# First layer's attention: VectorE scales a head's weights before the next head's mask and maximum, from the third step on; one pair's end moves a step

## The reference

```
qf = q * scale
s_own = where(causal, einsum(qf, k_own), NEG_INF)      # 8 heads, 256 x 256
p = softmax(s_own)
out = einsum(p, v_own)
attn = head_rms_norm(merge_heads(out), attn_out_g, 8)
```

## Time and profile before

| | us |
|---|---|
| three runs | 1297.15, 1297.38, 1300.36 |
| median | 1297.38 |
| the profiled execution, whole | 1299.01 |
| its span, first to last instruction | 1297.1 |
| TensorE busy | 1121.5 (86%) |
| VectorE busy | 670.1 (52%) |
| ScalarE busy | 550.3 (42%) |
| mean granted TensorE clock | 0.95 |

### The profile page before, as it was taken

How to read it: one execution, slowest core, us unless ns; L and a number is a source line. 1 busy time by engine, 2 the same in 40 slices (tenths; PEclk the granted TensorE clock), 3 DMA queues, 4 the chain that set the end, 5 groups by cost and what they waited for, 6 DMA issues and landing times.

```text
span 1297.1 us, 20055 instructions
## 1 busy us (share of the span) xinstructions
PE 1121.5 (86%) x8501; PEld 845.5 (65%) x8501; DVE 670.1 (52%) x1422; ACT 550.3 (42%) x1202; POOL 0.2 (0%) x4
## 2 busy tenths in 40 slices
PE   6999999876675775757889999999999979999997
PEld 4777678544242542424456767888887758888886
DVE  4565765211111110111167756998876867777765
ACT  4564554111111110111155665666654755666653
POOL 0000000000000000000000000000000000000000
PEclk9999999899797889889899999999999999999999
DMA  9996848999999999999997457677757515554500
GB/s 388 423 413 263 364 195 346 406 427 426 428 427 427 424 426 426 427 426 427 425 425 276 175 227 277 243 277 290 294 218 293 235 65 203 198 190 189 195 33 33
DMA packets 29847, 397.36 MB, mean 306 GB/s; under 512 B 3512, under 2 KB 4920, under 8 KB 5432
## 3 DMA queue, kind: packets, MB, share of 16 engines
q1 hardware_dynamic: 29320, 395.72, 74.8%
q10 hardware_dynamic: 432, 0.30, 0.1%
HBM read 394.97 MB, written 1.05 MB: 305 GB/s over the span
## 4 chain that ended last, share of the span: by engine, by line
PE 57%; DMA 23%; DVE 12%; ACT 6%; issue 2%; DVEq 0%; ACTq 0%; SPq 0%
PE ps L1217 17%; DMA ring<-in_w13b 15%; PE ps L1221 9%; PE ps L1211 4%; PE ps L1213 4%; PE ps L1212 4%; ACT mem L2006 4%; DMA mem<-in_w 4%; DVE memr L2533 4%; PE ps L1796 4%; DVE mem L2533 3%; PE ps L1732 3%; PE ps L1251 3%; ACT memr L2006 2%; DMA mem<-in_w13b 2%; PE ps L1832 2%
## 5 line engine op out<-in xcount | busy, mean ns | idle before, releaser
L2533 DVE TENSOR_TENSOR memr<-ring,memr 128x512 fp32r<-128x512 f32 x432 | 292.3, 689 | 158.7 <-ACT memr L2006 155.2
L2006 ACT ACTIVATE memr<-ring 128x512 fp32r<-128x512 f32 x432 | 266.1, 629 | 189.9 <-PE ps L1213 85.5
L1217 PE MATMUL ps<-memr 128*128 128x512 f32 x1056 | 275.4, 394 | 3.3 <-DVE memr L2533 2.0
L2006 ACT ACTIVATE mem<-ps 128x256 f32<-128x256 f32 (+5 forms) x294 | 121.4, 432 | 341.1 <-PE ps L1796 221.2
L1217 PEld LDWEIGHTS ps<-memr 128*128 128x128 f32 x1056 | 186.7, 189 | 36.5 <-DVE memr L2539 5.0
L1211 PE MATMUL ps<-memr 128*128 128x256 f32 (+2 forms) x504 | 175.8, 349 | 4.6 <-DVE memr L2533 3.4
L1213 PE MATMUL ps<-memr 128*128 128x256 f32 (+2 forms) x504 | 165.2, 328 | 0.0
L1212 PE MATMUL ps<-memr 128*128 128x256 f32 (+2 forms) x504 | 165.2, 328 | 0.0
L2533 DVE TENSOR_TENSOR mem<-mem,ps 128x512 f32<-128x512 f32 (+1 forms) x76 | 43.5, 572 | 233.9 <-ACT mem L2006 233.9
L1221 PEld LDWEIGHTS ps<-memr 128*128 128x128 f32 x1056 | 151.4, 190 | 16.5 <-DVE memr L2539 0.9
L1221 PE MATMUL ps<-memr 128*128 128x256 f32 x1056 | 156.9, 282 | 0.9 <-DVE memr L2539 0.5
(11 more groups left out here) (190 smaller groups left out, 1011.4 us busy)
## 6 DMA issues: line engine op xcount, KB each, us to landing
ring<-in_wpk SPq DMA_DIRECT2D x89, 2048.0 KB, 8.3
ring<-in_w13a SPq DMA_DIRECT2D x17, 2048.0 KB, 45.4
mem<-in_w13b SPq DMA_DIRECT2D x16, 2048.0 KB, 46.1
ring<-in_w SPq DMA_DIRECT2D x16, 2048.0 KB, 45.8
ring<-in_w13b SPq DMA_DIRECT2D x15, 2048.0 KB, 43.1
mem<-in_w SPq DMA_DIRECT2D x15, 2048.0 KB, 44.7
mem<-in_w13a SPq DMA_DIRECT2D x15, 2048.0 KB, 43.4
mem<-in_wpk SPq DMA_DIRECT2D x1, 2048.0 KB, 10.4
```

The costliest lines, as they stand in the source:

```text
L1217: return self.e.matmul(ps[:, 0:512], a[0], b[1], start=start, stop=stop)
L2006: return self.e.activation(out, src, f, **k)
L2533: return self.e.tensor_tensor(out, a, b, op)
```

## The change

From step 3 to step 8 `a0_weigh(step - 1)` is called ahead of `a0_scores(step)`; at steps 1 and 2 it stays behind it. `a0_weigh` acts on VectorE alone, so the queues of the other engines don't change by this. The pairs' ends move from steps 5, 7, 9, 11 to steps 5, 8, 9, 11: the second pair's end is called a step later, on all engines. No operation is added or removed.

```
     def attention_first(self):
+        ends = {5: 0, 8: 1, 9: 2, 11: 3}
         for step in range(12):
+            if 3 <= step < 9:
+                self.a0_weigh(step - 1)
             if step < 8:
                 self.a0_scores(step)
-            if 1 <= step < 9:
+            if 1 <= step < 3:
                 self.a0_weigh(step - 1)
             if 2 <= step < 10:
                 self.a0_turn(step - 2)
             if 3 <= step < 11:
                 self.a0_values(step - 3)
-            if step >= 5 and step % 2:
-                self.a0_end((step - 5) // 2)
+            if step in ends:
+                self.a0_end(ends[step])
             yield
```

## The result

Over 14 runs each the changed kernel took 1301.07 us (1299.88 to 1303.26), the kernel before 1298.71 (1297.15 to 1300.36). The ratio of the two is 1.0019, 95% interval 1.0012 to 1.0026: slower by some 2.4 us (1.6 to 3.4 by the interval), more than the measurement is uncertain and less than 0.3%. The forecast was 2.30 us slower. (Its 1299.7 was counted from the median of the three runs shown then; with more runs that median is 1.3 higher.)

What follows compares the result with a forecast made beforehand. A ScalarE-VectorE loop bounds steps 3 to 7, with TensorE's own work close behind. 3.25 us for the loop plus 0.35 for the moved sum less 1.30 of waiting gives 2.30 us: 1297.38 to 1299.7 us, range 1296.2 to 1302.2.

Steps and rivals of the forecast that it cites:

- Part 1: Steps 3 to 7: scaling ahead of the mask lengthens the ScalarE-VectorE loop by 0.65 us each, 3.25 us in all.
- the plain loop: ScalarE's exponentials and rounding, VectorE's low part, mask and maxima in turn: 3.76 us before, 4.41 forecast.
- The bound of 0: Lower bound on the scaling's cost per step, if the loop had slack that the chain doesn't show.
- The bound of 0.74: Upper bound in us on the scaling's cost per step, by the ends shown; 3.70 over five steps.
- Part 2: Second pair's end moved from step 7 to 8: TensorE's 1.30 us wait for head 7's weights disappears.
- TensorE's sum: Head 7's transposition 2.30 us late: 3.25 for the loop, 0.35 for the moved sum, less the 1.30 wait.
- The margin in step 9: Moved end's chain finishes 0.2 to 0.8 us before TensorE's third-pair sum at 192.1, so it doesn't hold up step 9.
- The way to the end: From head 7's transposition through the expert stage: the 2.30 us delay passes undiminished to the kernel's end.
- (a): Rival: slack in the loop makes the scaling free, head 7's transposition 0.94 us earlier; 1296.4 us, 10%.
- (b): Rival: the delay happens but the expert stage's DMA swallows it; 1297.4 us, 12%.
- (c): Rival: moved end gains nothing, its chain overruns into step 9; 3.6 us slower, 1301.0 us, 15%.
- (d): Rival: VectorE's low part comes after the scaling, which then runs in a wait; given no chance of its own.

Runs made afterwards that it cites:

- e1: Against the kernel before: scaling ahead of the mask as in the change, second pair's end left in step 7; ratio 1.0025, +3.2 us.
- e7: The changed kernel run again unaltered, against the kernel before; ratio 1.0022, +2.9 us.
- e4: Against the kernel before: scaling ahead of the mask in steps 3 to 5 only, pairs' ends as in the change; ratio 1.0011, +1.4 us.
- e8: Against the kernel before: only the second pair's end moved to step 8, repeated for a narrower interval; ratio 0.9993, -0.9 us.
- e2: Against the kernel before: only the second pair's end moved from step 7 to step 8; ratio 0.9993, -0.9 us.

## Why the prediction was right

**Part 1, 0.65 us for each of five steps.** It measured 0.66, and 3.28 to 3.32 in all where 3.25 was worked out; the plain loop turned in 168.61 - 164.21 = 4.40 us where 4.41 was named. The bound of 0 is excluded by the straight line over 0, 3 and 5 steps. The bound of 0.74 is excluded as well: five times that would be 3.70. The start-to-start distance of the row was the right price, not the lengths shown. The sentence of the Trainium skill weighed there (VectorE: DVE Perf Modes, The DRAIN you can't avoid) doesn't fit these operations: the mask starts at 167.38, before the 0.55 us shown for the scalings at 166.92 have passed. The prediction left out that the same section adds an exception, a next operation that isn't held starts earlier, and the trace agrees with that.

**Part 2, the moved end.** Alone it was to bring the transposition 0.94 earlier and brought it 1.0. In the changed kernel it turns the 3.3 of e1 into 2.3.

**TensorE's sum.** 2.30 late at head 7's transposition is what the second profile of the changed kernel shows, to the hundredth. The first shows 3.09, and there a term was missing: the sum took TensorE's durations at full clock, although it put new idle time in front of them, and let the slab of step 7 be done when the values of head 5 were due. A falling clock was named only as something of a later stage. By the same slip the wait before the values in step 8, named as a sign, is missing in the first profile; the second has it, 0.33 us. So the agreement of 2.30 with the 2.4 measured is closer than anything here can vouch for: the interval, 1.6 to 3.4 us, holds 2.30 and 3.09 alike.

**The margin in step 9.** VectorE's low part was to come between 191.3 and 191.9 on the clock of the kernel before. In the first profile it came at 190.63, which is 192.25 on that clock, with TensorE itself late; in the second (e7) at 189.61, which is 191.45. In both ScalarE then still waited 0.5 us for TensorE's third sum, so the cover held.

**The way to the end.** The delay at the expert stage's issue is that of the transposition within 0.1 us in all nine profiles, and the ratios follow it roughly: from -1.95 and -1.4 to 3.31 and 3.2. From that issue to the end of the span it is 1074.5 us in the kernel before and in the changed one, and 1074.1 to 1074.8 in six of the other profiles; e4 with 1075.4 and e8 with 1077.2 lost something later. DMA's long stretch swallowed nothing, because its own start moved.

**The rivals.** (a) is refuted by e1 and e4. What it builds on did happen: TensorE's waits before the transposition went down, from 3.1 us to 1.2. But waits of 2.8 us before the values took their place. (b) is refuted by the issue and the times. (c) is refuted by e2 and e8 with e1. (d) is refuted by VectorE's order in the rows above.

**What was off.** The absolute time, 1301.07, lies just above the range that the prediction gave the forecast itself, 1298.6 to 1301.0, because the kernel before is 1.3 us slower by its larger sample than by the first three runs. And a change of 3.9 us is not "about the least" that such runs can tell from none: 2.4 us were told from none, with an interval of 0.9 us to either side.

## What to carry to other kernels

Work that VectorE did while ScalarE computed for it was free here; the same work in front of what ScalarE waits for was paid at its full start-to-start distance, once per turn of the loop. Before serving the busiest engine's waits earlier, look whether the operation that is moved crosses a hand-over (one engine's result that another waits for) of a tighter loop. In such a loop, the gain lay in taking hand-overs out of it: moving one end (-1 us by the traces) or splitting the ends (-1.9).

## What was not expected of the hardware

TensorE's granted clock fell to half in every profile in which the loop was lengthened and TensorE's waits stayed open (both of the changed kernel, e1 and e4), after one wait of 1.56 to 1.96 us that followed a shorter one, and in none of the others, though the kernel before waits for 1.30. How long it stayed down differed between two executions of the same kernel, 6.8 and 3.4 us, and with it the cost in this stage, 0.8 or nothing; why it differed isn't shown. An execution can also carry such a stretch where nothing was changed: the one at about 40 us stands in two of the ten profiles, and there everything by step 3 comes 1.1 to 2.0 us later than in the other eight.
